# A two-block transformer forward pass in split precision: the gate and up projections of two feed-forward stages with both activation halves in one matmul

## The reference, cut to what matters

```python
D_MODEL = 1024; SEQ = 256; D_FF = 2816

def swiglu(h, w_gate, w_up, w_down):
    return (jax.nn.silu(h @ w_gate) * (h @ w_up)) @ w_down

# in each of the two layers, after the attention or convolution part
x = x + swiglu(rmsnorm(x, ffn_norm[i]), w_gate[i], w_up[i], w_down[i])
```

## Time and profile before

| | us |
|---|---|
| three timed runs | 1359.47, 1360.54, 1363.09 (median 1360.54) |
| the profiled execution, its own time | 1354.39 |
| its span, first to last instruction | 1353.1 |
| layer 0's feed-forward: first gate product on VectorE, first residual add after it | 167.1, 356.8 |
| layer 1's: the same | 532.7, 725.95 |

### The profile page before, as it was taken

One profiled execution on the slowest core, in us unless ns is written; L12 is line 12 of the kernel. 1 busy time (PEld: TensorE's weight loads), 2 busy tenths in 40 slices (PEclk: granted clock), 3 DMA queues, 4 the chain that ended last, 5 costly groups with the idle time before them and its releaser, 6 DMA issues.

```text
span 1353.1 us, 22353 instructions
## 1 busy us (share of the span) xinstructions
PE 1242.8 (92%) x9262; PEld 1185.6 (88%) x9262; DVE 757.5 (56%) x975; ACT 680.1 (50%) x994; POOL 650.1 (48%) x327
## 2 busy tenths in 40 slices
PE   4999999999878889999998997899998797999996
PEld 3899899999778778999998886889898696999996
DVE  5547743333473666333365562466832676788885
ACT  5554644444554646444445544546624655555553
POOL 5433754445652317444453434634423745566662
PEclk9899999999989979999999998899999798999999
DMA  8454555555553435555554443444432644455540
GB/s 303 141 175 154 191 198 181 183 183 181 179 186 124 140 110 194 180 186 183 181 169 153 159 140 109 144 151 138 145 105 98 233 159 155 158 180 179 185 172 32
DMA packets 59749, 220.36 MB, mean 163 GB/s; under 512 B 6672, under 2 KB 6928, under 8 KB 59136
## 3 DMA queue, kind: packets, MB, share of 16 engines
q1 hardware_dynamic: 59184, 216.43, 48.3%
q10 hardware_dynamic: 288, 2.10, 0.4%
q0 software_dynamic: 176, 0.39, 0.1%
HBM read 217.85 MB, written 1.05 MB: 162 GB/s over the span
## 4 chain that ended last, share of the span: by engine, by line
PE 75%; DVE 10%; ACT 7%; issue 3%; POOL 3%; DMA 0%; SPq 0%; ACTq 0%; DVEq 0%; POOLq 0%
PE PS L284 20%; PE PS L286 20%; PE PS L285 20%; PE PS L289 15%; ACT w_hi L795 4%; DVE w_lo L1296 2%; POOL w_lo L1874 2%; DVE ARENA L1834 1%; DVE SQ L1560 1%; DVE SQ L1304 1%; DVE ARENA L1549 1%; DVE ARENA L1381 1%; ACT ARENA L893 1%; DMA consts<-sq_consts 0%; DVE Y_lo L1310 0%
## 5 line engine op out<-in xcount | busy, mean ns | idle before, releaser
L1874 POOL TENSOR_TENSOR w_lo<-raw,w_hi 128x1024 fp32r<-128x1024 f32 x202 | 514.4, 2552 | 509.4 <-ACT w_hi L795 509.4
L795 ACT ACTIVATE w_hi<-raw 128x1024 fp32r<-128x1024 f32 x404 | 422.4, 1052 | 192.8 <-PE PS L286 150.0
L1296 DVE TENSOR_TENSOR w_lo<-raw,w_hi 128x1024 fp32r<-128x1024 f32 x202 | 298.1, 1477 | 251.9 <-ACT w_hi L795 251.9
L284 PE MATMUL PS<-Y_hi,w_hi 128*128 128x256 f32 x1240 | 359.7, 290 | 20.3 <-issue 9.0
L285 PE MATMUL PS<-Y_lo,w_hi 128*128 128x256 f32 x1240 | 356.1, 287 | 0.0
L286 PE MATMUL PS<-Y_hi,w_lo 128*128 128x256 f32 x1240 | 355.8, 287 | 0.0
L284 PEld LDWEIGHTS PS<-Y_hi,w_hi 128*128 128x128 f32 x1240 | 243.1, 196 | 26.1 <-issue 19.6
L285 PEld LDWEIGHTS PS<-Y_lo,w_hi 128*128 128x128 f32 x1240 | 243.3, 196 | 0.1
L286 PEld LDWEIGHTS PS<-Y_hi,w_lo 128*128 128x128 f32 x1240 | 243.2, 196 | 0.0
L284 PE MATMUL PS<-H_hi,w_hi 128*128 128x256 f32 x808 | 232.9, 288 | 7.5 <-DVE w_lo L1296 3.7
L286 PE MATMUL PS<-H_hi,w_lo 128*128 128x256 f32 x808 | 229.7, 284 | 0.0
(11 more groups left out here) (191 smaller groups left out, 1498.9 us busy)
## 6 DMA issues: line engine op xcount, KB each, us to landing
raw<-stream SPq DMA_DIRECT2D x404, 512.0 KB, 3.7
ARENA<-sgu_bc ACTq DMA_DIRECT2D x1, 1536.0 KB, 6.8
ARENA<-memT SPq DMA_DIRECT2D x1, 1024.0 KB, 5.0
X<-xT SPq DMA_DIRECT2D x1, 1024.0 KB, 13.0
ARENA<-ctxT SPq DMA_DIRECT2D x1, 1024.0 KB, 7.4
outT<-ARENA SPq DMA_DIRECT2D x2, 512.0 KB, 2.7
ARENA<-sgu_wT ACTq DMA_DIRECT2D x1, 512.0 KB, 7.7
V<-vec SPq DMA_DIRECT2D x1, 199.0 KB, 2.5
```

Source lines behind the costliest of these rows:

```text
L284: pe.matmul(o, wh, xh, start=start, stop=False, skip_group_check=True)
L795: act.activation(w_hi[n % RING][:], raw[n % RAW][:], ACT.Copy).then_inc(*mark("hi", n))
L1296: dve.tensor_tensor(w_lo[n % RING][:], raw[n % RAW][:], w_hi[n % RING][:], ALU.subtract).then_inc(*mark("lo_dve", n))
L1874: pool.tensor_tensor(w_lo[n % RING][:], raw[n % RAW][:], w_hi[n % RING][:], ALU.subtract).then_inc(*mark("lo_pool", n))
```

## The change

It concerns gate and up of the two plain feed-forward stages (88 slots). `H` and `Y` become one tensor each, with the high and the low half of a chunk side by side, 512 numbers. A new `tall_both` issues two matmuls for a chunk in place of three: high weight by the 512 numbers into the whole bank, and low weight by the high half into the bank's second half. The gate is then the sum of the bank's halves. VectorE adds them: one `tensor_reduce` for the gate into `GF[:, 0]`, after which the product with `RS` reads `GF` in place of PSUM; and one for up into `UF`, 256 columns of the scratch area, after which the product with the gated value reads `UF` in place of PSUM. Each product waits for its sum. A bank is released by the sum. All other stages read the halves of `H` and `Y` as before, now with a stride between chunks.

```diff
--- before.py
+++ after.py
@@ -87,6 +87,7 @@
     "scores_dve": ("sc_zero", "sc", "sc_sum"),
     "vs_dve": ("vs_stats", "vs_var", "vs_unit"),
     "x_added": ("x_add_even", "x_add"),
+    "ffn_dve": ("gate_sum", "up_sum"),
     "conv_dve": ("conv1", "conv2"),
     "zeroed": ("init", "cu_zero", "img_zero"),
     "spatial_dve": ("sg_bias", "sg_gated", "sg_lo"),
@@ -160,8 +161,8 @@
         w_hi = [sb(f"w_hi{r}", [P, D], F32R) for r in range(RING)]
         w_lo = [sb(f"w_lo{r}", [P, D], F32R) for r in range(RING)]
         X = sb("X", [P, KC, T])
-        H = (sb("H_hi", [P, KC, T], F32R), sb("H_lo", [P, KC, T], F32R))
-        Y = (sb("Y_hi", [P, KC, T], F32R), sb("Y_lo", [P, KC, T], F32R))
+        H_BOTH, Y_BOTH = sb("H", [P, KC, 2 * T], F32R), sb("Y", [P, KC, 2 * T], F32R)
+        H, Y = ((both[:, :, 0:T], both[:, :, T:2 * T], both[:]) for both in (H_BOTH, Y_BOTH))
         SQ = sb("SQ", [P, KC, T])
         RS = sb("RS", [P, 2, T])
         G = (sb("G_hi", [P, T], F32R), sb("G_lo", [P, T], F32R))
@@ -204,6 +205,7 @@
         CG, CU, CV = area(1024, MC, T), area(5120, MC, T + 2), area(6784, MC, T)
         KS, VS, QB1 = area(21760, MC, T), area(23296, TT, MAIN), area(0, KC, T)
         QM = [QP, QB1[:, MC:KC]]
+        UF = area(0, T)
         EXS, PTS = [area(8448, 8, T), area(11392, 8, T)], [area(10496, 4, 512), area(13440, 4, 512)]
         Y_MEM = [Y, H]
         NB = 3 * P
@@ -300,6 +302,18 @@
                         pe.wait_ge(*past(*ready[k]))
                     w = slice(k * P, (k + 1) * P)
                     last = mm3(o, w_hi[r][:, w], w_lo[r][:, w], h[0][:, k], h[1][:, k], k == 0, k == KC - 1)
+                last.then_inc(*mark("used", n))
+                n += 1
+
+            def tall_both(b, h, ready=None):
+                nonlocal n
+                r = slot()
+                for k in range(KC):
+                    if ready:
+                        pe.wait_ge(*past(*ready[k]))
+                    w = slice(k * P, (k + 1) * P)
+                    mm(PS[:, b], w_hi[r][:, w], h[2][:, k], k == 0, False)
+                    last = mm(PS[:, b, T:2 * T], w_lo[r][:, w], h[0][:, k], False, k == KC - 1)
                 last.then_inc(*mark("used", n))
                 n += 1
 
@@ -428,12 +442,12 @@
                 p = j % 2
                 claim(2 * p, 2 * p + 1)
                 assert n == gate_slot(l, j)
-                tall(PS[:, 2 * p, 0:T], H_of[l], ready)
-                emptied[2 * p] = [("gate", l, j)]
+                tall_both(2 * p, H_of[l], ready)
+                emptied[2 * p] = [("gate_sum", l, j)]
                 if side:
                     side.step()
-                tall(PS[:, 2 * p + 1, 0:T], H_of[l])
-                emptied[2 * p + 1] = [("hidden", l, j)]
+                tall_both(2 * p + 1, H_of[l])
+                emptied[2 * p + 1] = [("up_sum", l, j)]
                 if side:
                     side.step()
 
@@ -1421,14 +1435,19 @@
                     dve.wait_ge(*past("used", gate_slot(l, j)))
                     if j:
                         dve.wait_ge(*past("g_lo", l, j - 1))
-                    dve.tensor_tensor(GF[:, 0], PS[:, 2 * p, 0:T], RS[:, 0], ALU.mult).then_inc(*mark("gate", l, j))
+                    dve.tensor_reduce(GF[:, 0], PS[:, 2 * p].rearrange("p (a t) -> p t a", a=2), AX,
+                                      ALU.add).then_inc(*mark("gate_sum", l, j))
+                    dve.wait_ge(*past("gate_sum", l, j))
+                    dve.tensor_tensor(GF[:, 0], GF[:, 0], RS[:, 0], ALU.mult).then_inc(*mark("gate", l, j))
                     fill()
                     if side:
                         side.step()
                     dve.wait_ge(*past("used", up_slot(l, j)))
+                    dve.tensor_reduce(UF, PS[:, 2 * p + 1].rearrange("p (a t) -> p t a", a=2), AX,
+                                      ALU.add).then_inc(*mark("up_sum", l, j))
                     dve.wait_ge(*past("silu_rs", l, j))
-                    dve.tensor_tensor(GF[:, 1], PS[:, 2 * p + 1, 0:T], GF[:, 0],
-                                      ALU.mult).then_inc(*mark("hidden", l, j))
+                    dve.wait_ge(*past("up_sum", l, j))
+                    dve.tensor_tensor(GF[:, 1], UF, GF[:, 0], ALU.mult).then_inc(*mark("hidden", l, j))
                     fill()
                     if side:
                         side.step()

```

## The result

The changed kernel takes **1372.54 us** (median of four runs, 1371.37 to 1373.56) against 1360.66 for the kernel before in the same comparison (also four runs, 1359.47 to 1363.09). The ratio is **1.0085, 95% interval [1.0067, 1.0102]**: slower by 11.9 us. The forecast was 1377, slower, in a range of 1358 to 1390. The profiled execution took 1371.37 us, its span 1370.1.

The account below looks back on a forecast made before the run. TensorE sets the pace before; after the change the joint VectorE and GpSimd chain, 17.66 us a pair, becomes the bound. +7.3 (layer 0) and +9.1 (layer 1) make +16.4 on 1360.54: 1377 us, range 1358 to 1390.

Parts of the forecast that it names:

- The mechanism: Plain feed-forwards: products on two SBUF operands are held by GpSimd's `w_lo` of 2.40 us, tying block and weight chains.
- 17.66 us a pair: Feed-forward body: VectorE and GpSimd's chain for an even and an odd block, against 17.28 before and 16.87 TensorE needs.
- The start: Start of layer 0: first product held until 169.41 instead of 167.5; gate sums of blocks 1 and 2 near 175.7, 184.6.
- The sums: VectorE's 88 reduces of 512 PSUM numbers in the feed-forwards: 0.68 us each, 60 us in all, passing beside GpSimd.
- rival 4: Feed-forward sums: the strided sum is slow, up to 1.36 us, adding 28 us for 1405; chance 0.09.
- TensorE's saving: Gate and up slots: merging two matmuls saves 0.013 us a chunk, 9.1 us in all, not subtracted from the forecast.
- Layer 0: End of layer 0's feed-forward: last down starts 6.0 us later, plus 1.3 for 14 matmuls at slow clock; +7.3.
- Layer 1: End of layer 1's feed-forward, with side instructions: last down starts at 730.5 against 721.41; +9.1.
- The sum +16.4: Both feed-forwards: the +7.3 and +9.1 added, taking the profiled execution from 1354.39 to 1370.8 us.
- The step from the profiles to the medians: Whole kernel: the +16.4 us from the profile put on the median 1360.54, other stages at no cost, giving 1377.
- Rival 1: Feed-forward body: sums hide, products aren't held, TensorE sets the pace; 5 us faster, 1355; chance 0.12.
- Rivals 2 and 3: Feed-forward pairs: `G_lo` before GpSimd's second `w_lo`, 1363, chance 0.17; up product loses its race with `w_lo`, 1370, chance 0.10.

Follow-up runs that it names:

- psum_up: Changed kernel with the up sum written into PSUM (the gate's bank) and the up product reading it there; 1355.97 us, 0.9953 of the kernel before.
- half_fill: Changed kernel with GpSimd's `w_lo` cut to 512 of 1024 columns in the two plain feed-forwards, computation incomplete; 1345.44 us, a total not to be compared.
- first profile of before: First profiled execution of the unaltered kernel before; span 1353.1 us, median of its timed runs 1360.66 us.
- third profile of before: The kernel before, nothing changed, profiled a third time (one run); span 1361.8 us, time 1363.09 us.
- gate_psum: Changed kernel with only the gate's sum written into PSUM (the other up bank) and the gate product reading it there; 1378.44 us, 1.0132 of the kernel before.
- after_again: The changed kernel once more, nothing altered; 1372.74 us, 1.0099 of the kernel before.
- no_sums: Changed kernel without the sums, products reading only the bank's first half from PSUM, two of three partial products left out; 1349.00 us, 0.9917 of the kernel before.

## Why the prediction was right, and where it wasn't

- **The mechanism: right.** The up product on two SBUF operands is held by GpSimd's `w_lo`, and the joint chain, not the sums' 60 us, bounds the stage. Shown from both sides, by psum_up (other operand) and half_fill (shorter holder).
- **17.66 us a pair: 17.79.** Phase by phase, from the even gate sum: GpSimd's second `w_lo` ends 8.48 (walked: 8.53), `G_lo` 8.77 (8.81), the odd gate sum starts 8.86 (8.73), the odd up product ends 15.21 (15.07). All of the 0.13 arises at one place: I let the odd gate sum start 0.08 before `G_lo` has ended, as instructions on one engine do, but it waits for `G_lo` by semaphore and starts 0.09 after. TensorE's wait in each pair shows 0.5 us, forecast 0.8, and the held up products 1.83, where the list of signs said "near 2.5"; the walk itself gives 1.8 (from the end of the up sum near 13.2 to 15.07).
- **The start: right.** The first product was held for 1.67 us (167.43 to 169.10); the sums of blocks 1 and 2 start at 175.31 and 184.24, forecast 175.7 and 184.6, 0.4 too late.
- **The sums: right.** 688 and 684 ns on average; the stride of half a bank costs nothing beside the earlier trace rows. That a reduce of 2048 goes "at the same rate per number" was loosely read, 1.12 ns for 1.33, but the term was taken from the other row. With that rival 4 (a slow sum) is out.
- **TensorE's saving: mis-sized**, 4.9 us and not 9.1. In the changed kernel neither can be had, as the chain hides it, so the forecast doesn't suffer; TensorE's own pace is 17.05 a pair, not 16.87.
- **Layer 0: +7.3 forecast, +9.2 measured.** The last down starts at 360.57, forecast 359.7 (nine pairs of 0.13, less the 0.4 of the start), after 4.19 us idle, forecast about 4. The slow clock behind it is the term that was too small: I put 14 matmuls at the lower level, +1.3; the windows 360.5 to 363.5 and 363.5 to 366 show granted clocks of 0.50 and 0.54, the lower of the two levels (1.2 GHz), through the whole slot, and the delay grows by 2.3 between the last down's start and the residual add.
- **Layer 1: +9.1 forecast, +11.1 measured.** The pair with side work lasts 21.44, forecast 21.5. Block 20 lasts 11.13, forecast 10.1; its `G_lo` (731.57) is held too and takes 2.56 us. That is half of the 2.0 missing, and nine pairs of 0.13 are the rest.
- **The sum +16.4: near, for compensating reasons.** By the first profile of before the feed-forwards cost 20.3 us, 3.9 more than forecast, and the spans differ by 17.0, since 3.0 come back between a and b, where the granted clock is 0.91 in that profile and 0.96 in the changed kernel's.
- **The step from the profiles to the medians: the one that failed.** I put the difference of two profiles on the median, 1360.54, and costed all other stages at nothing, since they keep their instructions. They do, but not their time. Against the third profile of before the feed-forwards cost 18.3 us, the spans differ by 8.3, and the other 10.0 are 4.55 less in a, 2.7 less in b, 2.0 less ahead of L0 and some 0.9 elsewhere. The medians differ by 11.9. So the changed kernel loses some 18 to 20 us in its own stages and gains 6 to 10 (by the medians and by the later profiles of before) where nothing was changed; 1377 was 4.5 too high although the stages' own term was too low. That 1377 came so near is therefore partly luck. The stride of the activations, put at nothing, shows no cost in the changed kernel: the stretch between the feed-forwards takes 174.0 us for 173.8 to 174.4 before, and the one from L1 to a 334.6 for 334.7 to 335.2. That the profile shown was 6 us below its median I had noted; of the 31 runs of that kernel timed beside the experiments none is below 1359.2.
- **Rival 1 (the sums hide): not so here**, but psum_up makes its condition true and takes 1355.97 where I had 1355. The layers give only 1.6 to 3.6 us of that, so the agreement is partly luck.
- **Rivals 2 and 3 (the order at the lock, the race of the up product): refuted.** In all 18 even blocks from block 2 on that have no side work, GpSimd's second `w_lo` went before `G_lo`, and the up product started 0.17 to 0.19 us before `w_lo` and took its 0.43.
- **What stays open.** What decides how much of a and b runs at the lower level. The medians of gate_psum and after_spread, 6 and 7 us above the changed kernel's for feed-forwards within 1 us of its, suggest that it goes with the kernel; the executions of no_sums, 8 to 9 us apart, and the three profiles of before, that it changes within one kernel as well. No run here varies the moment at which these stages begin and nothing else.

## What to carry to other kernels

Before an operand of a VectorE instruction moves from PSUM to SBUF, look at what GpSimd does beside it: the cost isn't the instruction's 0.42 us but the rest of GpSimd's, 2.4 us, and above all that two chains become one. When a new intermediate is needed, let the first instruction write it to a free half bank of PSUM, and the reader stays free. To see what bounds a stage, move some of its side work: where that gains, there was slack to move it into; where it costs the same anywhere, that chain is the bound. Slack is used up block by block, so compare the distance of two blocks on each engine and not only the waits. And never add a difference of two single profiles to a median without a second profile of the kernel before.

## What the hardware showed beyond that

- **The lock goes by turns.** In the even block above, each engine has its next instruction on SBUF operands ready when the other's ends, and they alternate: up product (VectorE, to 204.90), `w_lo` (GpSimd), `w_lo` (VectorE, to 208.25), `w_lo` (GpSimd, to 210.51), `G_lo` (VectorE, to 210.80). None goes twice in a row, in any of the 18 even blocks named above. A held instruction of 256 columns ends 0.28 us after its holder, whether it shows 1.83, 2.62 or 1.08 us. The Trainium skill ("SBUF — State Buffer", SBUF: two separate sides) says that of a VectorE instruction with two SBUF inputs and a GpSimd instruction the one that starts first gets the shared ports for the whole instruction. The trace agrees on the whole instruction, and adds who comes next.
- **A reduce may write PSUM as cheaply as SBUF** (694 and 684 ns for 512 numbers), and a product that reads PSUM, with its other operand in SBUF, wasn't held once in psum_up: the 44 up products average 0.425 us, none above 0.43.
- **The times of matmuls don't add up across widths.** Three of 256 columns cost 0.360 us and one of 512 among its like 0.227, which would make 0.347 of one of each; in turn they take 0.353. The 0.227 is from a stage where weights and activations have changed places as operands, and no run tells the two causes apart.
- **The same code takes one of a few times.** Stage a took 14.1 to 14.4, 15.7, 17.2, 18.7 or 20.2 us, in steps of 1.5, stage b (half_fill aside) 194.2 to 194.9 or 197.1 to 197.2; the longer a, the lower the granted clock over it, from 1.00 down to 0.66. gate_psum is 1 us better than the changed kernel in its own stages and 5.7 worse in the median. So 0.4%, 6 us, between two versions says little unless their stages are compared too.
